# Retention strips computed in the previous layer's context pass, one gate tile moved forward, four modulation slices and one store moved back

## The reference, cut to what matters

```python
for l in range(2):
    hl, hc = modulate(rms_norm(x, norm1[l]), ...), modulate(rms_norm(xc, norm1[l]), ...)
    # one projection w_in for four branches: retention, gated linear attention, grouped-query, differential
    # retention: scores * gamma_h ** distance, both directions, 4 heads
    # merge: sum over branches of sigmoid(gate logits, 4 x 1024 columns) * (y_b @ w_branch[b]), then @ w_out
    x = x + g1 * y_l
    x = x + g2 * ((silu(conv3(h @ w_up_a)) * (h @ w_up_b)) @ w_down)       # and the same for xc in layer 0
    # g1, g2, shifts and scales: silu(c) @ w_mod[l] + b_mod[l]
```

## Time and profile before

| | |
|---|---|
| Median of 3 runs | 2947.17 us (2946.6 to 2949.71) |
| Profiled execution | 2955.57 us, its span 2953.7 us |
| PE busy | 2727.0 us, 92% of the span |
| DVE busy | 1343.2 us, 45% |
| ACT busy | 676.4 us, 23% |
| POOL busy | 1510.8 us, 51% |
| Chain that ended last | PE 78%, DVE 10%, POOL 4%, ACT 3%, DMA 3% |

### The profile page before, as it was taken

One profiled execution on the slowest core, in us unless ns is written; L12 is line 12 of the kernel. 1 busy time (PEld: TensorE's weight loads), 2 busy tenths in 40 slices (PEclk: granted clock), 3 DMA queues, 4 the chain that ended last, 5 costly groups with the idle time before them and its releaser, 6 DMA issues.

```text
span 2953.7 us, 38363 instructions
## 1 busy us (share of the span) xinstructions
PE 2727.0 (92%) x15748; PEld 2236.6 (76%) x15748; DVE 1343.2 (45%) x1794; ACT 676.4 (23%) x1160; POOL 1510.8 (51%) x1412
## 2 busy tenths in 40 slices
PE   5899989999988999999979997998989887999999
PEld 2788877867766878888868876886767656988877
DVE  4522166643566855555570235216643666522221
ACT  4311232122244521100020012122221245211110
POOL 3434457522412435656578325556834324488886
PEclk9999989999988999999989998999989888999999
DMA  7422411311311833333343362221212106533322
GB/s 247 150 65 87 114 38 51 88 45 45 109 36 52 261 95 107 115 114 115 115 118 99 101 200 54 80 64 44 75 40 65 50 26 208 149 97 96 98 86 81
DMA packets 378233, 286.25 MB, mean 97 GB/s; under 512 B 10395, under 2 KB 338751, under 8 KB 377548
## 3 DMA queue, kind: packets, MB, share of 16 engines
q1 hardware_dynamic: 375680, 280.96, 31.9%
q10 hardware_dynamic: 1612, 2.75, 0.3%
q0 software_dynamic: 768, 0.09, 0.0%
HBM read 254.40 MB, written 29.36 MB: 96 GB/s over the span
## 4 chain that ended last, share of the span: by engine, by line
PE 78%; DVE 10%; POOL 4%; ACT 3%; DMA 3%; issue 1%; ACTq 0%; SPq 0%; DVEq 0%; POOLq 0%
PE ps L462 17%; PE ps L463 16%; PE ps L464 16%; PE ps L687 4%; PE ps L618 3%; PE ps L1037 3%; PE ps L503 2%; PE ps L505 2%; PE ps L504 2%; PE ps L983 2%; POOL w_hi L1174 2%; PE ps L707 1%; POOL w_lo L1177 1%; DMA arena<-logits 1%; PE ps L814 1%
## 5 line engine op out<-in xcount | busy, mean ns | idle before, releaser
L1174 POOL TENSOR_TENSOR w_hi<-ring,tiny 128x512 fp32r<-128x512 f32 x516 | 591.0, 1145 | 1195.3 <-PE ps L464 612.4
L462 PE MATMUL ps<-hh,w_hi 128*128 128x512 f32 (+1 forms) x2288 | 852.2, 372 | 27.4 <-DVE hl L1704 13.5
L1177 POOL TENSOR_TENSOR w_lo<-ring,w_hi 128x512 fp32r<-128x512 f32 (+1 forms) x572 | 787.6, 1378 | 78.8 <-ACT w_hi L1348 38.1
L463 PE MATMUL ps<-hl,w_hi 128*128 128x512 f32 (+1 forms) x2288 | 825.9, 361 | 0.0
L464 PE MATMUL ps<-hh,w_lo 128*128 128x512 f32 (+1 forms) x2288 | 822.5, 359 | 0.0
L462 PEld LDWEIGHTS ps<-hh,w_hi 128*128 128x128 f32 x2288 | 446.7, 195 | 134.9 <-issue 37.5
L464 PEld LDWEIGHTS ps<-hh,w_lo 128*128 128x128 f32 x2288 | 446.7, 195 | 64.8
L463 PEld LDWEIGHTS ps<-hl,w_hi 128*128 128x128 f32 x2288 | 448.3, 196 | 59.5 <-issue 1.7
L503 PE MATMUL ps<-w_hi,hh 128*128 128x256 f32 (+1 forms) x544 | 157.8, 290 | 19.6 <-ACT arena L1328 11.8
L1328 ACT ACTIVATE arena<-ps 128x512 f32<-128x512 f32 (+3 forms) x130 | 75.9, 584 | 420.8 <-PE ps L464 409.4
L462 PE MATMUL ps<-ffh,w_hi 128*128 128x512 f32 x352 | 142.5, 405 | 20.4 <-POOL w_lo L1177 13.7
(11 more groups left out here) (234 smaller groups left out, 3857.0 us busy)
## 6 DMA issues: line engine op xcount, KB each, us to landing
ring<-in_w_in SPq DMA_DIRECT2D x118, 512.0 KB, 4.0
ring<-in_w_mod SPq DMA_DIRECT2D x96, 512.0 KB, 4.1
ring<-in_w_up SPq DMA_DIRECT2D x88, 512.0 KB, 4.8
ring<-in_w_down SPq DMA_DIRECT2D x48, 512.0 KB, 4.1
ring<-in_w_out SPq DMA_DIRECT2D x32, 512.0 KB, 4.2
logits<-arena SPq DMA_DIRECT2D x32, 384.0 KB, 2.3
arena<-logits SPq DMA_DIRECT2D x32, 384.0 KB, 3.6
ring<-in_w_down SPq DMA_DIRECT2D x24, 384.0 KB, 3.4
```

What stands on the lines that cost most here:

```text
L462: pe.matmul(acc, wh[:, offset + k], hi[:, n, x:y], start=n == 0, stop=False)
L463: pe.matmul(acc, wh[:, offset + k], lo[:, n, x:y], start=False, stop=False)
L1174: pool.tensor_tensor(wh[:, 0:count], w, one[:].unsqueeze(2).to_broadcast([P, count, P]), ALU.mult).then_inc(*up("w_lead", ("lead", key, j)))
L1177: pool.tensor_tensor(wl[:, 0:count], w, wh[:, 0:count].bitcast(F32), ALU.subtract).then_inc(*up("w_split", ("split", key, j)))
```

## The change

Seven edits, of one diff:

1. The strips of layer 1 are made in layer 0's dctx pass: on DVE `strip_begun(1, u)` and `strip_ended(1, u-1)` stand behind the residuals of context tiles 0 to 4, on ACT the sixteen exponentials stand between the two parts of the norm, with one unused root behind them. Layer 0's strips stay.
2. `ff` is laid out as a context half and a latent half, so that the strips' place is free once the latent down pass is over. DVE's product per tile in the up pass becomes two instructions in layer 0 (L2108). Roots and scaled tiles of the norm get places of their own.
3. In layer 1 the first gate tile of retention goes behind f1 and ahead of f2, in the chunk order, on PE and on ACT. The early gate tile is then the second one, and the pieces between retention's steps come from six tiles, not seven.
4. Slices 44 to 47 go behind the first chunks of down tiles 3 to 6, and DVE takes them behind the residuals of down tiles 2 to 5.
5. The sixth modulation sum goes from ahead of down tile 4 to behind dctx tile 3.
6. The context's squares get two buffers, not eight; DVE waits for the sum of squares u-2, and PE sums u-2 behind dctx tile u. Tiles 6 and 7 are summed behind the pass.
7. `x_kept` is issued behind the second gate tile of retention, not behind f3, in both layers.

```diff
+def opening_tiles(l, b):
+    return gate_tiles(l)[b][:1] if l > 0 and b == "ret" else []
...
                 order += [("f", l, b, n)] + slices_behind(l, b, n)
+                order += [("g", l, g) for g in opening_tiles(l, b) if n == BR[b]["nq"] - 1]
...
-            order += [("down", l, n // 3, n % 3)] + slices[2 * FT + n:2 * FT + n + 1]
+            order += [("down", l, n // 3, n % 3)] + (slices[2 * FT + n // 3 - 3:2 * FT + n // 3 - 2] if n % 3 == 0 and n >= 9 else [])
...
                             projection(("f", l, b, j), hh, hl, W[l] if is_q(b, j) else T, banks(), each=each)
+                            if j == BR[b]["nq"] - 1:
+                                for part in gate_parts(l, opening_tiles(l, b)):
+                                    gate_part(l, part)
...
-                    if l + 1 < DEPTH and u == 4:
-                        sum_of_modulation(l + 1, 5, 6, 7)
...
+                        if u == 3:
+                            sum_of_modulation(l + 1, 5, 6, 7)
...
+                        if u >= 2:
+                            sum_of_squares(1, 1, "second", u - 2)
-                    for k in range(KT):
+                    for k in (KT - 2, KT - 1):
                         sum_of_squares(1, 1, "second", k)
...
-            KEEP = [("f", 0, "ret", 3), ("f", 1, "ret", 3)]
+            KEEP = [("g", l, gate_tiles(l)["ret"][1]) for l in range(DEPTH)]
...
                     norm_of(1, 1, "first")
+                    for h in range(4):
+                        strip_exponentials(1, h)
+                    act.activation(unread_root, eps, ACT.Sqrt)
                     norm_of(1, 1, "second")
...
-                if part == "first" and u >= 2:
+                if (part == "first" or which == 1) and u >= 2:
                     dve.wait_ge(*at(("squ", l, which, part, u - 2)))
...
-                    dve.tensor_tensor(ff[:, c, 0:w], cu[:, 0:w], psum(key)[:, 0:w], ALU.mult).then_inc(*up("dve_free", ("free", key)))
+                    if w > LAT:
+                        dve.tensor_tensor(ff_ctx[:, c], cu[:, LAT:T], psum(key)[:, LAT:T], ALU.mult)
+                    dve.tensor_tensor(ff[:, c], cu[:, 0:LAT], psum(key)[:, 0:LAT], ALU.mult).then_inc(*up("dve_free", ("free", key)))
...
-                for kind, n, g, k in next_modulation(l)[2 * FT:]:
-                    modulation_step(n, g, k)
                 if l + 1 < DEPTH:
                     for u in range(KT):
                         residual_of(1, 1, "first", u)
+                        for key in next_modulation(l)[2 * FT + u - 2:2 * FT + u - 1] if u >= 2 else []:
+                            modulation_step(*key[1:])
                     norm_of(1, 1, "first")
                     for u in range(KT):
                         residual_of(1, 1, "second", u)
+                        if 1 <= u <= 4:
+                            strip_ended(1, u - 1)
+                        if u < 4:
+                            strip_begun(1, u)
```

More of the change, by code:

```diff
@@ L163, in gate_parts @@
     return [(g, s, j) for g in tiles for s in range(len(segs(W[l]))) for j in range(2)]
+def opening_tiles(l, b):
+    return gate_tiles(l)[b][:1] if l > 0 and b == "ret" else []
 def early_parts(l, b):
-    return gate_parts(l, gate_tiles(l)[b][:1])
+    n = len(opening_tiles(l, b))
+    return gate_parts(l, gate_tiles(l)[b][n:n + 1])
 def gate_plan(l, b, steps):
-    parts = gate_parts(l, gate_tiles(l)[b][0 if b == "after" else 1:])
+    parts = gate_parts(l, gate_tiles(l)[b][0 if b == "after" else len(opening_tiles(l, b)) + 1:])
     plan = [[] for _ in range(steps)]
@@ L191, in weight_chunks @@
                 order += [("f", l, b, n)] + slices_behind(l, b, n)
+                order += [("g", l, g) for g in opening_tiles(l, b) if n == BR[b]["nq"] - 1]
             for pair in token_pairs(b):
                 order += [("t", l, b, n) for n in pair] + slices_behind(l, b, len(BR[b]["feat"]) + pair[0] // 2)
-            order += [("g", l, g) for g in gate_tiles(l)[b]]
+            order += [("g", l, g) for g in gate_tiles(l)[b] if g not in opening_tiles(l, b)]
         order += [("g", l, g) for g in gate_tiles(l)["after"]]
@@ L293, in bass_hybrid_backbone @@
         one = tiny[:, 151:152]
+        unread_root = tiny[:, 148:149]
         rd = tiny[:, 152:184]
@@ L318, in squares_of @@
                 return sqb[which][:, k % 2, x:y]
-            lo = (8 + k) * T if which == 1 else 5 * T + CTX * k
-            return arena[:, lo:lo + CTX]
+            if which == 1:
+                return sq_late[:, k % 2]
+            return arena[:, 5 * T + CTX * k:5 * T + CTX * (k + 1)]
+        root_at = {(1, 1): arena[:, AREA - T:AREA], (0, 2): arena[:, 2 * T:3 * T], (1, 2): arena[:, 2 * T:3 * T]}
+        tb_at = {key: arena[:, o:o + 2 * T].rearrange("p (b t) -> p b t", b=2)
+                 for key, o in (((1, 1), 10 * T + 128), ((0, 2), 3 * T), ((1, 2), 3 * T))}
         x_scaled = arena[:, 16 * T:24 * T].rearrange("p (t d) -> p t d", t=NT)
@@ L1259, in decays, with strip_exponentials @@
                 act.activation(pp1, pp1, ACT.Ln, bias=1.0).then_inc(*up("act_set", ("softplus",)))
+            def strip_exponentials(l, h):
+                act.wait_ge(*at(("strip_in", l, h)))
+                act.activation(e0, e0, ACT.Exp)
+                act.activation(e1, e1, ACT.Exp, scale=-1.0)
+                c0, c1 = 8 * l + h, 8 * l + 4 + h
+                act.activation(strip[:, h, NEAR:], dist[:, 0:FAR], ACT.Exp, scale=lg[:, c0:c0 + 1], bias=lg_ctx[:, c0:c0 + 1])
+                act.activation(e2, dist[:, 0:FAR], ACT.Exp, scale=neg_lg[:, c1:c1 + 1],
+                               bias=lg_lat[:, c1:c1 + 1]).then_inc(*up("strip_exps", ("strip_exp", l, h)))
             def norm_of(l, which, part):
                 key, (x, y) = ("norm", l, which, part), PARTS[l, which][part]
+                rs, tb = root_at[l, which], tb_at[l, which]
                 act.wait_ge(*at(("full", key)))
@@ L1474, in _ @@
                             modulation_bias(columns_between(l)[b][slot // 2 - 1])
-                        if b == "ret" and j < 4:
-                            h = j
-                            act.wait_ge(*at(("strip_in", l, h)))
-                            act.activation(e0, e0, ACT.Exp)
-                            act.activation(e1, e1, ACT.Exp, scale=-1.0)
-                            c0, c1 = 8 * l + h, 8 * l + 4 + h
-                            act.activation(strip[:, h, NEAR:], dist[:, 0:FAR], ACT.Exp, scale=lg[:, c0:c0 + 1],
-                                           bias=lg_ctx[:, c0:c0 + 1])
-                            act.activation(e2, dist[:, 0:FAR], ACT.Exp, scale=neg_lg[:, c1:c1 + 1],
-                                           bias=lg_lat[:, c1:c1 + 1]).then_inc(*up("strip_exps", ("strip_exp", l, h)))
+                        if l == 0 and b == "ret" and j < 4:
+                            strip_exponentials(l, j)
                         if b in ("gqa", "dif") and 1 <= j <= nf:
@@ L2046, in _ @@
                 for b in ORDER:
-                    if b == "ret":
-                        strips(l)
+                    if b == "ret" and l == 0:
+                        for h in range(4):
+                            strip_begun(l, h)
+                            strip_ended(l, h)
                     if b == "gla":
```

32 lines of the change are left out of this document (19 added, 13 removed).

## The result

The changed kernel takes 2928.07 us (median of 6 runs, 2920.62 to 2930.82) beside 2953.96 us for the kernel before (6 runs, 2946.6 to 2961.34) in the same rounds. The ratio is 0.9913, 95% interval 0.9895 to 0.993: faster, by 25.9 us. Forecast were 2925.7 us, inside 2915 to 2937. The profiled execution has a span of 2926.5 us beside 2953.7, so 27.2 us less. The predicted time is nearly met, but partly by luck. The two errors nearly cancel. For the profiled execution the forecast was 2934.1 us.

A forecast was written before the change was run, and what follows sets the result against it. PE, busy for 92% of the span, was taken as the bound. Savings of 14.3 (layer 1's start) + 3.5 + 3.7 = 21.5 us off 2955.6 gave 2934.1, less 8.4 for the median 2925.7 us; range 2915 to 2937.

The forecast's parts named there:

- Strips: Start of layer 1: strips moved into the context pass save 10.0 us of wait and 2.3 of slow stretch, 12.3.
- The rival that they hold the residuals back: Context pass: strips delay DVE's residuals and PE waits for squares behind each tile; 2955 us, chance 0.04.
- Gate tile: Layer 1 before f2: 5.4 us of products fill the wait, f2 starts 4.3 later, a 0.9 bank wait goes.
- The rival that the norm isn't held back: Layer 1: slow norm pairs come from the 3 MB store, so f2 follows the gate tile; 2920 us, chance 0.17.
- That filler is missed: Layer 1's retention waits at steps without a gate piece and 5.4 us come back; 2931 us, chance 0.1.
- Squares: Context pass: 2.2 us of squares move into it, and f0 behind it starts 0.9 us later.
- Modulation sum: Moved from down pass to context pass: costs PE the same either place, same slow products behind it; 0 us.
- Slices: Start of layer 0's down pass: POOL's later splits run faster without slice products beside them; net 3.5 us saved.
- My marks for this stage: Start of down pass: PE restarts about 1 us sooner in tile 0, tile 1 begins 12 us after, not 15.
- Kept copy: Layer 0's first branch: the later copy lets the first token chunk land sooner; 3.7 us saved, layer 1 0.
- only layer 1 gains: POOL's splits stay the bound in down pass and layer 0's first branch; 2933 us, chance 0.1.
- the change does nothing: Whole kernel: the waits lie elsewhere than where the diff touches, so no gain; chance 0.04.

The follow-up runs named there:

- f3_late: Changed kernel with one wait added: in layer 1 POOL splits f3 only when ACT has written its last part of the norm; 2920.13 us, ratio 0.989.
- gate_back: Changed kernel with layer 1's early gate tile back at its old place, none ahead of f2; 2932.43 us, ratio 0.9924.
- keep_back: Changed kernel with the kept copy issued behind f3 again, in both layers; 2928.64 us, ratio 0.9923.
- slices_back: Changed kernel with the last four slices behind the first down chunks again and the modulation sum ahead of down tile 4; 2933.14 us, ratio 0.9926.
- down_late: Changed kernel with one wait added: SP issues layer 0's second down chunk only after DVE's first `ffl` of the down pass; 2924.18 us, ratio 0.9905.
- sum_spread: Changed kernel with the modulation sum's sixteen narrow products placed singly behind every other product of context tiles 4 and 5; 2925.72 us, ratio 0.9906.

## Why the prediction was nearly right, point by point

**Strips: 12.3 us forecast, 10.9 found** by undoing them, and by the earlier trace rows beside the waits after: 10.9 us are 0.9. All sixteen exponentials lie between 1676.6 and 1707.0, no PE wait in the pass is theirs. They began 28.2 us into the pass, as I had placed them, but a head took 9.0 us, not 10.6, so they ended 64 us into it and not 72. The rival that they hold the residuals back is refuted.

**Gate tile: 5.4 - 3.4 + 0.9 = 2.9 us forecast without f0's own delay, 5.7 found.** The mechanism is the one forecast, and f3_late shows it: POOL's split of f3 slows the last pairs of the norm. One step of its size was wrong. The two last pairs are slow by 1.7 us each, as forecast, 3.4 together; but f2 waits only for ACT's last part of the norm, which stands behind the first operation of the last pair, and not for the second. So f2 comes 1.7 + 0.7 = 2.4 us later behind f0 (19.37 against 16.97), as ACT's last part does (18.3 us behind f0 against 15.9 in gate_back). The wait before f2 was 2.7 us, not 4, and the slow stretch 3 us, not 5. And 1.1 us at the masked scores (4.4 to 3.3) were not in the sum; they come with one gate tile and go with none or two, and why wasn't followed further. 5.4 - 2.4 + 0.9 + 1.1 are 5.0 of the 5.7; the rest is within what the clock does to this stage (gate_back above). The rival that the norm isn't held back is refuted as to its cause by keep_back: the 3 MB store does nothing to it. Its condition, the freed pairs, is what f3_late brings about, and is worth 2.3 to 5.2 us up to the first token products, of the 5.7 it named. That filler is missed is refuted: retention shows no new wait with one tile or with two.
The Trainium skill, "SBUF — State Buffer", section "SBUF: two separate sides", has the lock of the port pair that DVE and GpSimd share. The pairs of 1.15 + 1.50 us beside a split against 0.5 + 0.5 with POOL idle agree with it. It has the lock held for one instruction; the shut-outs of 7.1 to 13.0 us, over many DVE instructions of 0.68 us, go beyond that.

**Squares: f0 0.9 us later forecast.** 2.16 more in the pass, 1.29 less behind it: 0.87. Right.

**Modulation sum: 0 forecast; -1.8 us in the profiled execution, +1.6 in others.** It costs 6.92 us in the pass where the clock falls behind it and 5.73 - 2.16 = 3.57 where it does not, and had cost 5.16. "The same in either place, with the same slow products behind it" was right for the work, not for the clock.

**Slices: 3.5 us forecast, 7.28 and 5.87 found.** Here a step failed: "That stays; it is why PE waits 8.55." It did not stay. I had taken the shut-out as a property of the pair (an unbroken DVE chain locks POOL), where it depends on when POOL asks. Without slice 44 behind the first down chunk, the second chunk landed 2.2 to 3.4 us after POOL's last operation instead of 4.6 to 4.7, and POOL got its turns. slices_back restores the old state, down_late restores the shut-out with the slices left in their new place. My marks for this stage failed too: PE has no restart at 1534.5 and tile 1 no 12 us behind it; PE waits 5.11 us at the start and then at most 0.83 us at a time, 8.2 us in all, for `ffl` alone, where before waited 4.2 + 11.4 = 15.6 us. With the longer wait ahead of tile 0 taken off, the 7.28 and 5.87 us are 6.4 and 5.8.

**Kept copy: 3.7 us forecast, 4.7 and 4.8 found,** 5.35 by undoing it. PE's wait fell from 7.08 to 1.86, and the slow stretch behind it went, which the sum had left out as a bound. The chunk landed 3.2 us sooner, in 5.28 us and not the 4 to 5 I had marked; 2.0 more came from POOL's four operations on it, where I had expected DVE to slow them as before. In layer 1, 0 as forecast.

**The sum.** Found in the two executions of the changed kernel: 4.67 + 7.28 + 5.30 - 9.08 + 1.29 + 18.40 = 27.9, and 26.6 us, beside 21.5 forecast. Of the 6 us missing, 2.4 to 3.8 are the slices, 1 the copy, and the rest the start of layer 1 (1.29 + 18.40 - 2.16 = 17.5 against 14.3). The modulation sum takes 1.8 off again. The other stages took 0.6 and 6.1 us back in these executions. That only layer 1 gains is refuted by f-t and d0-d1; that the change does nothing, by the ratio's interval.

## What to carry to other kernels

Look at how two engines that share a resource met in the trace, not only how long each took: a split that was shut out for 12.7 us was freed by moving a transfer elsewhere, without touching either engine's work. When filler is moved into a wait, ask what its own preparation (here POOL's split) now runs beside; holding that split back by one wait gave another 2 to 5 us up to the first token products. Where untouched stages scatter by more than the effect, undo one part at a time and compare stages between landmarks, and profile the same kernel twice before explaining a few us.

## What the runs showed of the hardware that was not expected

- DVE's chain of 22 subtractions, each with two SBUF inputs, either shuts POOL's split out to its end (POOL operations of 7.1 to 13.0 us, DVE 0.68 us each) or takes turns with it (POOL 1.04 to 1.61 us, DVE 1.52 and 1.77 us). All 17 cases with POOL idle for 4.0 us or more beforehand were of the first kind, all 42 with 3.4 us or less of the second. Whether POOL's idleness decides or the time for which DVE has run undisturbed, which in these chains is much the same, stays open: no run separates them.
- Taking turns costs DVE 24 to 25 us for what takes 13.3 us alone, and was still the better case for PE: tile 1 began 5.8 to 7.3 us sooner behind tile 0 than in before.
- The granted clock falls to half behind short PE waits or narrow products in some executions and not in others of the same program. The block of narrow products was followed by such a stretch in 5 of 9 executions, worth up to 3.35 us, and the stage from f0 to G gained 18.4 us in the changed kernel, its repeat and sum_spread, and 21.2 to 21.4 us in keep_back, slices_back and down_late, with the same waits before f2 and the scores.
